# First modulation and first three projection units in two halves of the features

## The reference, cut to what matters

```python
def ada_modulation(cond, w, b):
    m = jax.nn.silu(cond) @ w + b
    return m.reshape(m.shape[:-1] + (6, D_MODEL))

def modulate(x, shift, scale):
    return x * (1 + scale) + shift

# first layer: u = modulate(x, shift, scale) for latent and context tokens, then
#   u @ w_in        w_in is 1024 x 2336, split into attention and recurrence parts
```

## Time and profile before

| | us |
|---|---|
| median of 3 runs | 2299.51 (2298.7 to 2300.08) |
| profiled execution, its time | 2300.38 |
| its span | 2298.5 |
| TensorE busy | 2174.1 (95%) |
| VectorE busy | 807.6 (35%) |
| mean granted TensorE clock | 0.981 of full |

### The profile page before, as it was taken

How to read it: one execution, slowest core, us unless ns; L and a number is a source line. 1 busy time by engine, 2 the same in 40 slices (tenths; PEclk the granted TensorE clock), 3 DMA queues, 4 the chain that set the end, 5 groups by cost and what they waited for, 6 DMA issues and landing times.

```text
span 2298.5 us, 27962 instructions
## 1 busy us (share of the span) xinstructions
PE 2174.1 (95%) x10576; PEld 1049.9 (46%) x10576; DVE 807.6 (35%) x1709; ACT 405.3 (18%) x864; POOL 360.6 (16%) x386
## 2 busy tenths in 40 slices
PE   6999998999998999999997999999998999999996
PEld 3546545777554343334432444444553343334432
DVE  2694214556626311111111633434455111111114
ACT  2301142554211111010111410100111100110112
POOL 0000012222122100101000423221321010201003
PEclk8999999999999999999999999999999999999998
DMA  9892000001425999999998411114326999999997
GB/s 388 329 370 80 1 0 1 2 2 38 149 92 208 394 419 419 420 411 419 411 420 352 172 37 55 37 55 163 142 110 266 416 419 419 405 419 419 414 395 297
DMA packets 135816, 572.50 MB, mean 249 GB/s; under 512 B 25049, under 2 KB 38521, under 8 KB 93690
## 3 DMA queue, kind: packets, MB, share of 16 engines
q1 hardware_dynamic: 123002, 537.04, 58.9%
q0 software_dynamic: 12672, 33.57, 3.7%
HBM read 548.52 MB, written 34.62 MB: 254 GB/s over the span
## 4 chain that ended last, share of the span: by engine, by line
PE 79%; DMA 7%; DVE 6%; SPq 4%; issue 3%; ACT 1%; DVEq 0%; POOLq 0%; ACTq 0%
PE bank L1284 21%; PE bank L1360 12%; PE bank L1308 10%; PE bank L864 10%; PE bank L1199 5%; PE bank L1156 5%; DMA bigA<-in_moe_w 4%; SPq L543 3%; PE bank L815 3%; DVE lnwb L1777 2%; PE bank L950 1%; PE bank L967 1%; PE bank L1420 1%; PE bank L1141 1%; PE bank L981 1%
## 5 line engine op out<-in xcount | busy, mean ns | idle before, releaser
L1284 PE MATMUL bank<-bigA,bigB 128*32 128x512 f32 (+2 forms) x1888 | 479.7, 600 | 15.4 <-DMA bigA<-in_moe_w 10.6
L864 PE MATMUL bank<-bigC,bigB 128*128 128x512 f32 (+3 forms) x768 | 292.8, 537 | 0.0
L1284 PEld LDWEIGHTS bank<-bigA,bigB 128*32 128x32 f32 (+2 forms) x1888 | 157.8, 133 | 237.6 <-issue 230.0
L1308 PE MATMUL bank<-bigA,bigB 128*32 128x512 f32 (+2 forms) x912 | 242.5, 594 | 3.6 <-DVE bigB L2222 3.1
L864 PEld LDWEIGHTS bank<-bigC,bigB 128*128 128x128 f32 x768 | 142.4, 192 | 128.0 <-issue 119.8
L1284 PE MATMUL bank<-bigC,bigB 128*32 128x512 f32 (+2 forms) x560 | 171.4, 593 | 0.0
L1360 PE MATMUL bank<-bigB,bigA 128*128 128x512 f32 x384 | 170.7, 592 | 0.0
L1474 ACT ACTIVATE bigB<-bank,small 128x128 f32<-128x128 f32 x280 | 104.6, 460 | 369.8 <-PE bank L815 369.7
L2542 POOL DMA_INDIRECT y_rows<-bigB,ints x42 | 42.4, 1010 | 810.5 <-DVE bigB L2227 790.3
L2218 DVE TENSOR_TENSOR bigB<-bigB,bank 128x512 f32<-128x512 f32 x42 | 28.9, 688 | 306.4 <-PE bank L1284 306.4
L2227 DVE TENSOR_TENSOR bigB<-bank,gate 128x512 f32<-128x512 f32 x84 | 54.1, 686 | 234.3 <-PE bank L1308 234.3
(11 more groups left out here) (347 smaller groups left out, 2623.6 us busy)
## 6 DMA issues: line engine op xcount, KB each, us to landing
bigA<-in_moe_w SPq DMA_DIRECT2D x250, 1024.0 KB, 24.6
bigC<-in_moe_w SPq DMA_DIRECT2D x80, 1024.0 KB, 23.3
bigA<-in_ada_w SPq DMA_DIRECT2D x40, 1024.0 KB, 6.8
misc<-in_moe_w SPq DMA_DIRECT2D x36, 1024.0 KB, 24.1
lnwb<-in_moe_w SPq DMA_DIRECT2D x18, 1024.0 KB
bigA<-y_rows SPq DMA_DIRECT2D x14, 1024.0 KB, 11.9
bigA<-in_w_in_odd SPq DMA_DIRECT2D x12, 1024.0 KB, 5.4
bigA<-in_ada_w SPq DMA_DIRECT2D x4, 2048.0 KB, 13.8
```

Source lines behind the costliest of these rows:

```text
L864: last = mm(bank(n % 3)[:, 0:w], uT[:, k, t * P:(t + 1) * P], wring[:, g % 2, k, at_:at_ + w], start=(k == 0), stop=(k == KC - 1))
L1284: last = mm(bank(m)[at_:at_ + w, :], xT[:, j, KC // 2 * h + k, at_:at_ + w], w13_at(SLOT_OF[m, h, q][0], k), start=(h == 0 and k == 0), st ...
L1308: last = mm(bank(6 + n)[at_:at_ + w, :], gT[:, 2 * h + k, at_:at_ + w], w2_at(SLOT_OF[2, h, q][0], k)[:, n * 512:(n + 1) * 512], start=(h ...
```

## The change

The 1024 features of x are taken in two halves, 0 to 511 and 512 to 1023, and a block of 128 features is now contiguous (before, feature p * 8 + k stood at partition p of block k). The eight blocks are kept.

- Transfers: the first weights come in eight parts of 1 MB, four for the shift and scale of the first half and four for the second, in runs of 2 KB. w_in(0) comes in two halves of 1 MB, one behind each four. x tiles 1 and 2 come before the second four. The bias of the two results comes as one row, ahead of all.
- Row products: each half is 16 matmuls (two for each k), which use two of the four groups of 32 partitions at a time; the bias is two matmuls of one row. The columns of a half are 4 matmuls of 128 x 4. The second half's semaphores are shared by two parts each, and both waits are for both.
- TensorE's order: rows of the first half, x_T of tile 0 (its first half), columns, first half of unit 0; then parts 0 and 1 of the second half's rows, x_T of tile 1, first half of unit 1, parts 2 and 3; then the rest of x_T and of units 0 to 2, interleaved, with x_T(3) before the second half of unit 2. From unit 3 on it is as before.
- ada_part(0) waits for the first half's rows, ada_part(1) for the second half's.
- The places of the first sixteen partial_T are half a unit earlier; the last four stay.
- VectorE modulates tiles 0 and 2, ScalarE tile 1, each in halves.
- Some semaphores are merged: h_out and out_done to rows_out, rms_a and sd to root, bias_in to const_in, wa2_zero to dve_step, with the counts changed to fit. This part of the diff is left out.

```diff
-        ada_first = at(bigA, 0, KC, 2 * D)
-        mrow = lnwb[:, 0:512]
+        ada_first = at(bigA, 0, 2, 4, KC // 2, 512)
+        mrow = lnwb[:, 0:1024].rearrange("p (h n) -> p h n", h=2)
+        first_bias = bigC[0:1, 4096:4096 + 2 * D]
...
-        sums_after = {8 + 3 * (i // 2) + i % 2: i for i in range(20)}
+        HALVED = 3
+        sums_after = {7 + 3 * (i // 2) + i % 2 + (i >= 16): i for i in range(20)}
...
-                    sp.wait_ge(S("u_T"), t - 2)
+                    sp.wait_ge(S("u_T"), t + 1)
...
+            load(first_bias, T["ada_b"][0:1, 0:2 * D], "cond_in")
+
+            def first_part(h, n):
+
+                k, m = 4 * (n // 2), n % 2
+                load(ada_first[:, h, n], ada_k[0][:, k:k + 4, D * m + 512 * h:D * m + 512 * h + 512],
+                     f"ada_half{n % 2}" if h else f"ada_in{n}")
+
+            def w_in(g, k0=0, k1=KC):
+                lo, w = groups[g]
+                if g >= 2:
+                    sp.wait_ge(S("proj_mm"), last_unit[g - 2] + 1)
+                load(wring[:, g % 2, k0:k1, 0:w], T["w_in_even"][0].rearrange("(k p) n -> p k n", k=KC)[:, k0:k1, lo:lo + w],
+                     "w_half" if k1 < KC else f"w_in{g % 2}")
+
             for n in range(4):
                 if n == 3:
                     x_tile(0)
-                load(ada_first[:, 2 * n:2 * n + 2, :], ada_k[0][:, 2 * n:2 * n + 2, 0:2 * D], f"ada_in{n}")
+                first_part(0, n)
                 if n == 0:
                     load(cst[:, 0:C_FIRST], T["const_f"][:, 0:C_FIRST], "const_in")
-                    load(biasc[:, 0, 0:2], ada_bias(0)[:, 0:2], "bias_in")
-
-            def w_in(g):
-                lo, w = groups[g]
-                if g >= 2:
-                    sp.wait_ge(S("proj_mm"), last_unit[g - 2] + 1)
-                load(wring[:, g % 2, :, 0:w], T["w_in_even"][0].rearrange("(p k) n -> p k n", k=KC)[:, :, lo:lo + w],
-                     f"w_in{g % 2}")
+            w_in(0, 0, KC // 2)
+            x_tile(1)
+            x_tile(2)
+            for n in range(4):
+                first_part(1, n)
+            w_in(0, KC // 2, KC)
...
             def ada_part(n):
-                if n == 0:
-                    sp.wait_ge(S("ada_mm"), 1)
+                if n < 2:
+                    sp.wait_ge(S("ada_mm"), 1 + 2 * n)
                 if n >= 4:
...
-            w_in(0)
-            x_tile(1)
-            x_tile(2)
...
-            for k in range(KC):
-                if k % 2 == 0:
-                    pe.wait_ge(S(f"ada_in{k // 2}"), 16)
-                for n in range(4):
-                    last = mm(bank(0)[32 * n:32 * n + 32, :], cond[:, k, :], ada_first[:, k, n * 512:(n + 1) * 512],
-                              start=(k == 0), stop=(k == KC - 1))
-            last.then_inc(S("ada_mm"), 1)
             pe.wait_ge(S("const_in"), 16)
-            pe.wait_ge(S("cond_a"), 2)
-            for k in range(KC):
-                for h in range(2):
-                    last = mm(bank(1)[64 * h:64 * h + 64, 4 * k:4 * k + 4], cols(mrow)[:, k, :], cc("pick")[:, 4 * h:4 * h + 4],
-                              start=True, stop=True)
-            last.then_inc(S("ada_mm"), 1)
-
-            def u_ready(t):
-                pe.wait_ge(S("u_ev"), t + 1 if t < 2 else 2 * t)
-                if t < 2:
-                    pe.wait_ge(S("u_ev_d"), t + 1)
+            pe.wait_ge(S("cond_in"), 48)
+
+            def first_rows(h, q0, q1):
+
+                if h and q0 == 0:
+                    pe.wait_ge(S("cond_a"), 2)
+                for m in range(2 if q0 == 0 else 0):
+                    mm(bank(3)[32 * m:32 * m + 32, :], cc("ones")[0:1, 0:32], first_bias[:, m * D + 512 * h:m * D + 512 * h + 512],
+                       start=True, stop=False, skip_group_check=True)
+                for q in range(q0, q1):
+                    m = q % 2
+                    pe.wait_ge(S(f"ada_half{q % 2}" if h else f"ada_in{q}"), 32 if h else 16)
+                    for k in range(4 * (q // 2), 4 * (q // 2) + 4):
+                        n = 2 * (k % 2) + m
+                        last = mm(bank(3)[32 * n:32 * n + 32, :], cond[:, k, :], ada_first[:, h, q, k % 4, :],
+                                  start=(k == 1), stop=(k >= KC - 2), skip_group_check=True)
+                if q1 == 4:
+                    last.then_inc(S("ada_mm"), 1)
+
+            def first_columns(h):
+
+                pe.wait_ge(S("cond_a"), 2 + h)
+                for k in range(4):
+                    last = mm(bank(7)[:, 16 * h + 4 * k:16 * h + 4 * k + 4], mrow[:, h, k * P:(k + 1) * P], cc("pick")[:, 0:4],
+                              start=True, stop=True, skip_group_check=True)
+                last.then_inc(S("ada_mm"), 1)
+
+            def u_ready(t, h=1):
+                if t >= HALVED:
+                    pe.wait_ge(S("u_ev"), 2 * t - 2)
+                elif t == 1:
+                    pe.wait_ge(S("u_ev"), h + 1)
+                else:
+                    pe.wait_ge(S("u_ev_d"), 2 * h + t // 2 + 1)
+
+            def x_T_half(t, h):
+
+                if h == 0:
+                    pe.wait_ge(S(f"x_in{t}"), 16)
+                else:
+                    u_ready(t, 0)
+                for k in range(4):
+                    last = tp(bank(4 + t)[:, k * P:(k + 1) * P], xring[t][:, (4 * h + k) * P:(4 * h + k + 1) * P], ident)
+                last.then_inc(S("u_T"), 1)
             def x_T(t):
                 pe.wait_ge(S(f"x_in{t % 3}"), 16 * (t // 3 + 1))
-                if t >= 2:
-                    u_ready(t - 2)
-                transposes(xring[t % 3], 4 + 2 * (t % 2)).then_inc(S("u_T"), 1)
+                u_ready(max(t - 2, HALVED - 1))
+                for k in range(KC):
+                    last = tp(bank(4 + 2 * (t % 2) + k // 4)[:, (k % 4) * P:(k % 4 + 1) * P], xring[t % 3][:, k * P:(k + 1) * P], ident)
+                last.then_inc(S("u_T"), 1)
+
+            def unit_half(t, h):
+
+                if t == 0:
+                    pe.wait_ge(S("w_in0" if h else "w_half"), 16)
+                u_ready(t, h)
+                lo, w = unit_cols(0, t)
+                for k in range(4 * h, 4 * h + 4):
+                    last = mm(bank(t)[:, 0:w], uT[:, k, t * P:(t + 1) * P], wring[:, 0, k, 0:w], start=(k == 0), stop=(k == KC - 1),
+                              skip_group_check=True)
+                if h:
+                    last.then_inc(S("proj_mm"), 1)
...
-            x_T(0)
-            x_T(1)
-            for n in range(len(units)):
-                unit(n)
+            first_rows(0, 0, 4)
+            x_T_half(0, 0)
+            first_columns(0)
+            unit_half(0, 0)
+            first_rows(1, 0, 2)
+            x_T_half(1, 0)
+            unit_half(1, 0)
+            first_rows(1, 2, 4)
+            x_T_half(2, 0)
+            x_T_half(0, 1)
+            x_T_half(1, 1)
+            first_columns(1)
+            unit_half(2, 0)
+            x_T_half(2, 1)
+            unit_half(0, 1)
+            unit_half(1, 1)
+            x_T(HALVED)
+            unit_half(2, 1)
+            for n in range(HALVED - 1, len(units)):
+                if n >= HALVED:
+                    unit(n)
                 if n + 2 < NTC:
                     x_T(n + 2)
...
-            act.wait_ge(S("cond_in"), 32)
+            act.wait_ge(S("cond_in"), 48)
             go(condx, craw, ACT.Exp, scale=-1.0).then_inc(S("cond_a"), 1)
-            act.wait_ge(S("ada_mm"), 1)
-            go(mrow, bank(0), ACT.Copy).then_inc(S("cond_a"), 1)
-            act.wait_ge(S("cond_ok"), 2)
+            for h in range(2):
+                act.wait_ge(S("ada_mm"), 1 + 2 * h)
+                go(mrow[:, h], bank(3), ACT.Copy).then_inc(S("cond_a"), 1)
+                act.wait_ge(S("cond_ok"), 2 + h)
+                shift, scale = mod_of(0, 0)
+                act.wait_ge(S("u_T"), HALVED * h + 2)
+                for k in range(4):
+                    last = go(uT[:, 4 * h + k, P:2 * P], bank(5)[:, k * P:(k + 1) * P], ACT.Identity,
+                              bias=shift[:, 4 * h + k:4 * h + k + 1], scale=scale[:, 4 * h + k:4 * h + k + 1])
+                last.then_inc(S("u_ev"), 1)
             def u_tile(t):
-                act.wait_ge(S("u_T"), t + 1)
+                act.wait_ge(S("u_T"), t + 1 + HALVED)
                 dst, mod = parts(uT[:, :, t * P:(t + 1) * P]), mod_of(0, 0, int(t >= NT))
                 modulated(dst, 4 + 2 * (t % 2), mod, "u_ev")
-                if t >= 2:
-                    modulated(dst, 4 + 2 * (t % 2), mod, "u_ev", 4, KC)
-
-            u_tile(0)
-            u_tile(1)
+                modulated(dst, 4 + 2 * (t % 2), mod, "u_ev", 4, KC)
...
-            dve.wait_ge(S("bias_in"), 16)
-            dve.wait_ge(S("ada_mm"), 2)
-            for j in range(2):
-                V(v.scalar_tensor_tensor(modc[:, j], bank(1)[:, 0:32].rearrange("p (k m s) -> p m k s", m=2, s=2)[:, j], float(j),
```

(20 more changed lines are left out.)

43 lines of the change are left out of this document (21 added, 22 removed).

## The result

| | before | after |
|---|---|---|
| time, median (lowest to highest), us | 2299.54 (2298.16 to 2302.41) | 2302.97 (2300.62 to 2304.86) |
| profiled execution: time, span, us | 2300.38, 2298.5 | 2303.69, 2301.7 |
| TensorE, share of the span / of the chain that ended last | 95% / 79% | 95% / 76% |
| transfers, share of the chain that ended last | 7% | 9% |
| first vector sum (T0), us | 72.47 | 75.28 |

The ratio is 1.0014, 95% interval 1.0008 to 1.002: 3.4 us slower, which is inside the 0.2% that the prediction drew as its bound. Lines answer to lines like this: row products L829 are L851, short transposes L815 are L879 (half a tile) and L886 (a whole one), half units L896, units L864 are L914, partial_T L876 is L926, the reduction L1766 is L1841.

What follows compares the result with a forecast made beforehand. The prediction took VectorE's chain of sums as the bound, its start T0 shifting the whole run. T0 +3.8, after it +0.2 and clock +0.5 summed to +4.5 us: 2304.9 against the profiled execution, given as 2304.0, range 2298.5 to 2310.

Steps and rivals of the forecast that it cites:

- T0: Start of VectorE's chain, its first vector sum: forecast at 76.3 against 72.47, +3.8 us, shifting the whole run.
- The first half unit: TensorE's start of unit 0's first half: about 23 to 24.6, some 12 us before the old 36.1.
- The rate of 2 KB runs: First weights' transfers: 388 GB/s instead of 424 with 8 KB runs, so 1.05 MB takes 2.70 us, not 2.48.
- The shared wait: Second half's first row products: two-part semaphores hold TensorE for parts 0 and 2 until 31.2, 1 and 3 until 33.9.
- g: Time the second half's rows are done, releasing ring part 1's transfer: 44.5, bounds 42.5 and 51.
- From g to x tile 3: Transfers restarting on an empty queue: x tile 3 lands 17.2 us after g, at 61.7, where it was 51.9.
- From x tile 3 to x tile 4: Transfers: x tile 4 comes 6.2 us after x tile 3, not 4.3, a new TensorE wait of 1.9.
- After T0: VectorE's chain behind its first sum: TensorE waits of 1.3, 0.4 and 1.2, 2.9 against 2.7, so +0.2 us.
- The clock: TensorE's idle time before x tile 3 may drop its clock: 1 us at half a chance, +0.5 us.
- The lower clock through the second rows: Rival: second half's row products run at the low clock; g 48.5, T0 80.3, 2308.0, up to 2311 us; chance 0.28.
- The queue never runs dry: Rival: second rows done before about 36, transfers without gap; x3 at 54.2, T0 68.8, 2296.0 us; chance 0.10.
- No shift at all: Rival: unseen room in VectorE's chain absorbs a 3 us delay of T0; 2299.5 to 2300.5 us; chance 0.10.

Runs made afterwards that it cites:

- the experiment made for it: Kernel before with its first weights loaded as sixteen transfers in 2 KB runs, not four in 8 KB runs: 2300.84 us, ratio 1.0009.
- the pairs in order of arrival: Changed kernel with the second half's shared semaphores pairing parts 0 and 1, 2 and 3, not 0 and 2, 1 and 3: 2298.59 us, ratio 0.9994.
- the filled wait: Changed kernel with four added matmuls, results unused, in TensorE's wait for x tile 3: 2303.09 us, ratio 1.0017.
- the halves without the earlier sums: Changed kernel with the transposed sums back at their places in the kernel before: 2307.01 us, ratio 1.0032.
- the version with the half unit first: Changed kernel with x_T and unit 1's first half ahead of all the second half's rows: 2299.38 us, ratio 1.0; run again unchanged, 2299.49 us.

## Why the prediction was right

**The first half unit** was put at 23 to 24.6: 23.19. **The rate of 2 KB runs**, 388 GB/s: 387 to 400 in the stretches from 12 to 35, and 388 in the experiment made for it. **The shared wait**: q = 0 was to start at 31.2 and q = 1 at 33.9; q = 0 starts at 30.85, behind a wait that a transfer ends, q = 1 at 33.6, and both are done at 35.8. The experiment with the pairs in order of arrival shows it from the other side: the same 16 products run in 1.94 us from 30.80.

**g**, 44.5 predicted, was 43.6. The term in it that was mis-sized most is the last: for q = 2 and 3 I took the middle, 2.6 us, between running together (1.7) and in turn (3.4). They ran together (16 records in 1.94 us). The other is the 0.5 for a slow first half unit: it was slow, 5.37 us, and still ended before the data came. Against these two stands the second half unit, 3.70 us and not 3.4.

**From g to x tile 3**, 17.2: measured 17.0 (43.6 to 60.61), with the queue empty from 37.5 on, where the prediction had 37 or 38. **From x tile 3 to x tile 4**, 6.2: 6.23 (60.61 to 66.84). The wait of 1.9 for x tile 4 isn't in the row, since the slow half unit took its place; the filled wait brought it out as 1.68. **T0**: 76.3 predicted, 75.28 measured, and the 1.0 is g's 0.9 and 0.2 of the way to x3.

**After T0**, +0.2: the last sum moved 3.00 with T0's 2.81. The waits of TensorE behind the sums that I put at 1.3, 0.4 and 1.2 are 0.98, 0.53 and 1.41 in VectorE's rows, 2.9 both times. The prediction left TensorE about 1 us of its late waits; 1.97 are left, the 3.16 us of the earlier trace rows are gone. That cost nothing and gave nothing, since the end of the chain is VectorE's.

**The clock**, +0.5 for half a chance of a slow restart that costs 1 us: in the profiled execution of after it fell and cost 0, in three others 1.0. So the size was right, and that after's profile shows none of it is luck. Sum +4.5, measured +3.3 by the profiled executions: 1.0 of the difference is T0, 0.5 the clock, and 0.3 were added behind the last sum.

**The rivals.** *The lower clock through the second rows* (g 48.5, 2308): the clock did fall, the stretch 31:35 has 0.59, but it was up again from 34.3, before the second half unit (3.70 us, full speed), as the point that speaks against this rival had it: a slow first half unit is busy longer (to 28.5). That it was this that brought the clock back in time wasn't tried. In the profile of the halves without the earlier sums the first half unit is as slow (5.37 us) and the clock is full all through these rows, so the fall there isn't in every execution. *The queue never runs dry* was the right mechanism in the wrong kernel: in after it did run dry for 8 us; with the rows at 37.3 it nearly didn't, and T0 came to 70.2 to 71.6, where the rival said 68.8, and to 2299.5 us, where it said 2296. The step in it that failed is x tile 3 at 54.2 (55.4 to 56.1 measured): the queue still has a weak spot, 225 and 131 GB/s in 37:38 and 38:39 of the version with the half unit first, and 193 and 8 in its second execution. *No shift at all* fell with T0, last sum and span moving together.

What I did not see is the size of what was compensated. The prediction treated the earlier sums as a term inside T0 (4.3 us earlier in position) and never priced them alone. Priced alone, they are a version of before at 2296.25 us.

## What to carry to other kernels

A start that came 13 us earlier was worth nothing here, since the instruction that frees the next buffers came later. Look for the first transfer in an in-order queue that waits for the moved work, and put that work first, since all that is queued behind pays. When a change has two parts, price each alone; here one gained 3.7 us and the other lost 7.4, and the sum hid both. Before filling a wait to keep the clock up, compare when the next transfer lands with when TensorE comes to it: here that difference, 0 to 1.0 us, was all that there was to gain. And don't read a gain of 1 or 2 us from one profile when a clock step falls in the stretch.

## What the runs showed of the hardware

- Row products into different groups of 32 partitions, each behind a wait of its own, still overlap when they are neighbours in TensorE's program and their data is there: 16 records in 1.94 us in the second lot of after, 32 in 3.66 in the version with the half unit first. So the row products of the halves cost no more each than those of before (16 in 1.92) when they stand together; when waits separate them, 8 records take 1.91, twice as long each.
- Transfers in runs of 2 KB moved 386 to 388 GB/s, one transfer of 2 MB as well as pieces of 0.5 MB, and in runs of 8 KB 424, on the same queue.
- The same eight products at the same place of the same kernel took 3.67 us in one execution and 5.37 in another: the granted clock was full beneath them in the one and fell to 1.2 GHz beneath them in the other. The clock's fall to 1.2 GHz in or after a wait of 3.7 to 4.9 us for x tile 3 cost 0, 0.2 or 1.0 us in five profiles.
